# Crossing the inner layer's pieces two visits later, and multiplying two down chunks by turns

## The reference

```
h2 = rms_norm_2(x, norm2_w[l])
x = x + (silu(h2 @ w_ffn_gate[l]) * (h2 @ w_ffn_up[l])) @ w_ffn_down[l]
return rms_norm_2(x, norm_f_w)
```

## Time and profile before

| | |
|---|---|
| median of 3 runs | 2250.62 us (2250.55 to 2250.92) |
| profiled execution | 2248.62 us, its span 2247.3 us |
| TensorE busy | 2215.1 us, 99% of the span |
| DVE busy | 1532.2 us, 68% |
| ACT busy | 1217.1 us, 54% |
| mean transfer rate | 190 GB/s |

### The profile page before, as it was taken

How to read it: one execution, slowest core, us unless ns; L and a number is a source line. 1 busy time by engine, 2 the same in 40 slices (tenths; PEclk the granted TensorE clock), 3 DMA queues, 4 the chain that set the end, 5 groups by cost and what they waited for, 6 DMA issues and landing times.

```text
span 2247.3 us, 29098 instructions
## 1 busy us (share of the span) xinstructions
PE 2215.1 (99%) x11384; PEld 1826.7 (81%) x11384; DVE 1532.2 (68%) x2032; ACT 1217.1 (54%) x1681; POOL 115.3 (5%) x101
## 2 busy tenths in 40 slices
PE   9999999999999999999999999999999999999998
PEld 7888888888888887878788888887887888788776
DVE  5677765757765677675665556768886488855875
ACT  5546665646665654554454555555554345544553
POOL 0003210002220121000000000000000000000000
PEclk9999999999999999999999999999999999999999
DMA  7456676656686764445644456666756656665663
GB/s 259 145 169 182 188 211 224 206 169 195 185 242 206 215 188 137 147 131 169 206 150 152 148 170 223 212 210 185 236 188 208 198 183 207 212 208 182 192 226 131
DMA packets 311305, 426.79 MB, mean 190 GB/s; under 512 B 118976, under 2 KB 119136, under 8 KB 311040
## 3 DMA queue, kind: packets, MB, share of 16 engines
q1 hardware_dynamic: 309008, 417.82, 58.6%
q0 software_dynamic: 1584, 6.16, 0.9%
q10 hardware_dynamic: 576, 0.95, 0.1%
HBM read 396.06 MB, written 2.10 MB: 177 GB/s over the span
## 4 chain that ended last, share of the span: by engine, by line
PE 87%; DVE 5%; issue 3%; ACT 3%; DMA 2%; POOL 1%; SPq 0%; DVEq 0%; ACTq 0%; POOLq 0%
PE ACC L1091 21%; PE ACC L1093 20%; PE ACC L1092 20%; PE ACC L983 3%; PE ACC L984 3%; PE ACC L985 3%; PE SCPV L983 2%; PE SCPV L985 2%; PE SCPV L984 2%; DVE WL L2216 2%; ACT WH L1120 1%; ACT arena L1120 1%; PE SCPV L605 1%; DMA W<-in_a_w_in 0%; PE SCPV L998 0%
## 5 line engine op out<-in xcount | busy, mean ns | idle before, releaser
L2216 DVE TENSOR_TENSOR WL<-W,WH 128x1024 fp32r<-128x1024 f32 x729 | 895.2, 1236 | 423.6 <-PE ACC L1093 187.7
L1120 ACT ACTIVATE WH<-W 128x1024 fp32r<-128x1024 f32 x729 | 745.3, 1050 | 267.5 <-PE ACC L1093 128.6
L1091 PE MATMUL ACC<-WH,XH 128*128 128x512 f32 x1888 | 765.3, 405 | 3.3 <-ACT arena L1120 2.4
L1093 PE MATMUL ACC<-WH,XL 128*128 128x512 f32 x1888 | 737.6, 391 | 0.0
L1092 PE MATMUL ACC<-WL,XH 128*128 128x512 f32 x1888 | 735.9, 390 | 0.0
L1091 PEld LDWEIGHTS ACC<-WH,XH 128*128 128x128 f32 x1888 | 355.0, 188 | 80.2 <-issue 5.1
L1093 PEld LDWEIGHTS ACC<-WH,XL 128*128 128x128 f32 x1888 | 354.4, 188 | 76.2
L1092 PEld LDWEIGHTS ACC<-WL,XH 128*128 128x128 f32 x1888 | 355.4, 188 | 68.8 <-issue 1.2
L1091 PE MATMUL ACC<-WH,HH 128*128 128x512 f32 x328 | 129.5, 395 | 3.2 <-DVE HL L1663 2.1
L1092 PE MATMUL ACC<-WL,HH 128*128 128x512 f32 x328 | 128.3, 391 | 0.0
L1093 PE MATMUL ACC<-WH,HL 128*128 128x512 f32 x328 | 128.1, 390 | 0.0
(11 more groups left out here) (368 smaller groups left out, 2392.5 us busy)
## 6 DMA issues: line engine op xcount, KB each, us to landing
W<-in_w_in SPq DMA_DIRECT2D x84, 1024.0 KB, 5.0
W<-in_a_w_in SPq DMA_DIRECT2D x47, 1024.0 KB, 5.2
W<-in_w_ffn_gate SPq DMA_DIRECT2D x44, 1024.0 KB, 5.9
W<-in_w_ffn_up SPq DMA_DIRECT2D x44, 1024.0 KB, 5.3
W<-in_w_ffn_down SPq DMA_DIRECT2D x44, 1024.0 KB, 5.1
W<-in_b_w_in SPq DMA_DIRECT2D x40, 1024.0 KB, 5.2
W<-in_a_w_out SPq DMA_DIRECT2D x16, 1024.0 KB, 5.9
W<-in_b_w_out SPq DMA_DIRECT2D x16, 1024.0 KB, 6.3
```

The source lines that it names most:

```text
L1091: MM(out, hx, WH[:, k, 0:ch.width], start=q == 0 and k == 0, stop=False)
L1093: ins = MM(out, lx, WH[:, k, 0:ch.width], start=False, stop=last and k == QK - 1)
L1120: return nc.scalar.activation(out, in_, func, **how)
L2216: TT(tiles_of(M.WL[K.pair(n)], ch, half), raw, tiles_of(M.WH[n % 3], ch, half).bitcast(F32), ALU.subtract).then_inc(*did("weights_rest", n ...
```

## The change

`halves` of the feed-forward pieces starts at the fourth visit behind its piece's chunk instead of the second, and `joined` at the eleventh instead of the ninth. Through the formula above the crossing moves one load back in SP's order. The first two down chunks of each part become one chunk `d.p{p}c01` of twice the quads: for each piece of the part first the quad of the columns 0 to 511, which accumulates in ACC0 and ACC1, then that of the columns 512 to 1023, in SC0 and SC1. So a piece is first wanted two quads after the one before it, not one. The last piece crosses by DMA like the others. The squares and gains of the final norm for the first two column groups start behind the joint chunk, one visit apart.

```
-BY_DMA = {... "h0.d": range(4), "h1.d": range(4), "h2.d": range(2)}
+FF_STARTS = (0, 4, 8)
+BY_DMA = {... "h0.d": range(4), "h1.d": range(4), "h2.d": range(3)}
...
-        for c in range(NC_D):
-            add(f"d.p{p}c{c}", one("w_ffn_down_2", c * CH), "dve", quads=n, row0=done * CH, xs="H", fresh=f"h{p}.d" if c == 0 else None)
+        add(f"d.p{p}c01", one("w_ffn_down_2", 0), "both", quads=2 * n, row0=done * CH, xs="H", fresh=f"h{p}.d")
+        for c in (2, 3):
+            add(f"d.p{p}c{c}", one("w_ffn_down_2", c * CH), "dve", quads=n, row0=done * CH, xs="H")
...
-                begin(after(f"d.gu{done + j}") + 1, "halves", f"h{p}.d", j)
-                begin(after(f"d.gu{done + j}") + 8, "joined", f"h{p}.d", j)
+                begin(after(f"d.gu{done + j}") + 3, "halves", f"h{p}.d", j)
+                begin(after(f"d.gu{done + j}") + 10, "joined", f"h{p}.d", j)
...
-    for c in range(NC_D - 1):
-        begin(after(f"d.p2c{c}"), "squares", "f", c)
-        begin(after(f"d.p2c{c}") + 3, "gained", c)
+    for c, n in ((0, "d.p2c01"), (1, "d.p2c01"), (2, "d.p2c2")):
+        begin(after(n) + c % 2, "squares", "f", c)
+        begin(after(n) + 3 + c % 2, "gained", c)
...
+                        if j in FF_STARTS[1:]:
+                            pe.wait_ge(*at("acc_taken_dve", f"d.p{FF_STARTS.index(j) - 1}c1", t))
...
+    def both(ch, visit, taken):
+
+        hi, lo, last_pair = M.hi["H"], M.lo["H"], FF_STARTS[int(ch.name[3])] + ch.quads // 2 - 1
+        for q in range(ch.quads):
+            n, kq, c = ch.first + q, q // 2, q % 2
+            WH, WL = M.WH[n % 3], M.WL[K.pair(n)]
+            for half in range(QK // HK):
+                pe.wait_ge(*at("weights_rest", n, half))
+                if c == 0:
+                    pe.wait_ge(*at("turned", ch.fresh, 2 * kq + half))
+                for t in range(TB):
+                    if q == 0 and half == 0:
+                        pe.wait_ge(*at(*taken[t], t))
+                    if q == 1 and half == 0:
+                        pe.wait_ge(*at("up_taken", last_pair, t))
+                    out = (M.ACC, SC)[c][t][:, :]
...
+            visit = both(ch, visit, taken)
+            taken = [("acc_taken_dve", ch.name[:-2] + "0")] * TB
...
+    def both_taken(ch, c, t):
+        dve.wait_ge(*at("multiplied", ch.first + ch.quads - 2 + c, 1, t))
+        x = M.X[:, t, c * CH:(c + 1) * CH]
+        TT(x, (M.ACC, SC)[c][t][:, :], x, ALU.add).then_inc(*did("acc_taken_dve", f"{ch.name[:-2]}{c}", t))
...
+                    if ch.taker == "both" and q >= ch.quads - 2 and half == 1:
+                        both_taken(ch, q % 2, t)
```

More of the change, by code:

```diff
@@ L38 @@
 FF_PARTS = (4, 4, 3)
+FF_STARTS = (0, 4, 8)
 WARM = (10, 22)
-BY_DMA = {key: range(NC_D) for key in ("go.a", "x.b", "go.b", "x.c", "mx.c", "x.d")} | {"h0.d": range(4), "h1.d": range(4), "h2.d": range(2)}
+BY_DMA = {key: range(NC_D) for key in ("go.a", "x.b", "go.b", "x.c", "mx.c", "x.d")} | {"h0.d": range(4), "h1.d": range(4), "h2.d": range(3)}
 PROBS_SPLIT, PROBS_READ = 8, 17
@@ L480, in sp_program @@
                 sp.wait_ge(*at("weights_rest", n - 3, 1))
-            row = ch.row0 + (q // 2 if ch.taker == "pair" else q) * QK * P
+            row = ch.row0 + (q // 2 if ch.taker in ("pair", "both") else q) * QK * P
             place = 0
-            for w, col, width in [("w_ffn_up_2", *ch.parts[0][1:])] if ch.taker == "pair" and q % 2 else ch.parts:
+            second = {"pair": [("w_ffn_up_2", *ch.parts[0][1:])], "both": [("w_ffn_down_2", CH, CH)]}
+            for w, col, width in second[ch.taker] if ch.taker in second and q % 2 else ch.parts:
                 src = a[w][0][row:row + ch.tiles * P, col:col + width].rearrange("(k p) n -> p k n", p=P)
@@ L1032, in pair @@
         return visit + 1
+    def both(ch, visit, taken):
[13 more added lines that the diff above has]
+                    out = (M.ACC, SC)[c][t][:, :]
+                    for k in range(half * HK, (half + 1) * HK):
+                        x = kq * QK + k
+                        hx, lx = hi[:, x, t * P:(t + 1) * P], lo[:, x, t * P:(t + 1) * P]
+                        MM(out, hx, WH[:, k, :], start=x == 0, stop=False)
+                        MM(out, hx, WL[:, k, :], start=False, stop=False)
+                        ins = MM(out, lx, WH[:, k, :], start=False, stop=x == ch.quads // 2 * QK - 1)
+                    ins.then_inc(*did("multiplied", n, half, t))
+                    sides_of(tasks, K.starts, visit, live)
+                    visit += 1
+        return visit
     visit, taken = 0, [None] * TB
@@ L1075, in pe_program @@
             taken = [("gate_taken", int(ch.name[4:]))] * TB
+            continue
+        if ch.taker == "both":
+            visit = both(ch, visit, taken)
+            taken = [("acc_taken_dve", ch.name[:-2] + "0")] * TB
             continue
```

## The result

The changed kernel takes 2229.5 us in the median (2228.49 to 2230.15, 4 runs) against 2250.59 us before (2249.37 to 2250.92, 4 runs): a ratio of 0.9907, with a 95% interval of 0.989 to 0.9924. The forecast was 2231.4, in a range of 2229.5 to 2240, so the median lies on the lower end of the range; two of the four runs (2228.49 and 2229.42) lie under it. The profiled execution took 2230.15 us, the most of the four; its span is 2228.8.

The account below looks back on a forecast made before the run. TensorE, busy 99% of the span, was taken to bound the kernel. Savings of 8.2 + 2.6 + 0.4 + 8.0 = 19.2 us gave 2229.4, plus 2.0 for the median: 2231.4 us, range 2229.5 to 2240.

Parts of the forecast that it names:

- What bounds: TensorE, busy 99% of the span, bounds the kernel at 0.2267 us per matmul; only its standing still or added work matters.
- Edit one: Halves two visits later lets ACT round the third quad first; ten TensorE waits for the weights' rest go, 8.2 us.
- The crossing behind a load: On SP's queue the crossing, one load later, lands 5.5 us after issue, within margins of 2.4 and 1.8 us; cost 0.
- the serial bound: Crossing served only after the load ahead has wholly landed: 1660.25 us behind piece 2, still costing nothing by the margins.
- Edit two: Two down chunks by turns: two waits for HL go, 2.6 us, and slower starts at chunk changes, 0.4 us.
- Edit three: Last piece crossing by DMA removes TensorE's 5.5 us wait, eight transposes and slow clock; 8.0 us together.
- The sum: All gains on TensorE together: 8.2 + 2.6 + 0.4 + 8.0 = 19.2 us.
- The last step, from 2229.4 to 2231.4: Turned the profiled execution's forecast into the runs' median by adding the 2.0 us it lay above before.
- the range that I called likeliest: The forecast case's own range for the median, 2230 to 2233 us; chance 0.77.
- The weights' rest that stays late: Rival: another wait takes over in the third quads, so the halves shift gives 0, total 2239.6 us; chance 0.07.
- the waits that hid something slower: Rival: TensorE's waits were cover for something slower, such as the loads, so no change; chance 0.04.
- The slow load: Rival: each crossing waits for a load landing 8.5 us after issue, costing 28 us, total 2259; chance 0.03.

Follow-up runs that it names:

- e1: Kernel before with nothing but halves and joined two visits later; 2245.23 us, ratio 0.9979.
- e3: Changed kernel with halves and joined of the inner layer back at the second and ninth visit; 2238.97 us, ratio 0.9948.
- e5: Changed kernel with halves at the third visit instead of the fourth and joined at the tenth; 2229.04 us, ratio 0.9908.
- e8: Changed kernel with halves at the sixth visit instead of the fourth and joined at the thirteenth; 2228.99 us, ratio 0.9907.
- e7: Changed kernel with the inner layer's crossings taken by SP one load later still, behind two loads; 2264.07 us, ratio 1.0059.
- e2: Changed kernel keeping the joint chunks alone: halves and joined where they were before, last piece turned by TensorE; 2246.99 us, ratio 0.9985.
- e4: Changed kernel with the last piece turned by TensorE again, at the second visit behind its chunk; 2237.98 us, ratio 0.9943.
- e6: Changed kernel with the last piece turned by TensorE at the tenth visit behind its chunk; 2229.6 us, ratio 0.991.

## Why the prediction was right

**What bounds.** The pace of 0.2267 us from start to start held through every variant wherever the clock was granted in full, so that losses could be counted place by place. This was the step on which all else stood.

**Edit one, 8.2 us.** Shown by e1 (all ten waits go) and e3 (they come back, with an eleventh): 9.1 us at 11 places, 0.83 each where I had 0.82. The cause is the order on ACT, as e5 beside e3 shows: with the crossing where it had been in SP's order and `halves` only one visit later the gain is the same. The weights' rest had 1.5 us to spare, for 1.4 worked out.

**The crossing behind a load, 0.** Shown: e5 puts it ahead of the load again and is no faster. In the change the crossings landed after 4.7 to 6.3 us, where I took 5.5 and set 6.9 as the bound. Behind piece 2 `HL`'s first half ended at 1660.82 + 0.65 = 1661.5, 2.9 us before the fifth quad (1664.37). At the last piece, where `HL` is wanted that early, the margin was 2.6 us; I had 1.8:

```profile
2173.44 1.28 DVE L1699 TENSOR_TENSOR HL<-turning,HH 128x512 fp32r<-128x512 f32 x2
...
2176.72 0.39 PE L1058 MATMUL ACC<-WH,HH 128*128 128x512 f32 x1
```

The Trainium skill says that a queue's descriptors are taken in ring order on each DMA engine ("DMA: Bandwidth & Descriptors", Queues, rings and completion order). The medians fit that: 4.3 us with no load close ahead (e5) and behind one 3.6 us old (e8), 4.8 behind one 2.4 us old, 8.7 behind two. But the serial bound, which the prediction drew from that rule, did not hold in the change: by it the crossing behind piece 2 would have landed at 1650.23 + 5.3 + 4.3 = 1659.8, and it landed at 1657.4. The order costs nothing in the change because of the margin; in e7 it costs everything that was gained and more.

**Edit two, 3.0 us.** e2: 2.8 in the runs, 2.5 in the trace. That the last pieces' wait grows when the shift is made without the joint chunk is e1's. The edits need each other: edits one and two together, which is e4, gave 11.9 us, while each alone gave 4.6 and 2.8.

**Edit three, 8.0 us.** e4: 8.5 from median to median (2237.98 less 2229.5), 9.2 when each is taken against its own runs of before (21.1 less 11.9), 9.4 in the trace. The part that varies is how long the clock stays low. e6 splits it.

**The sum.** 19.2 us forecast, 19.7 in the trace's stretch, 21.1 in the medians. The profiled executions' stretches agree with the sum to half a microsecond. The other 1.4 us of the medians was not located: the layers ahead vary without a change (the first `pair` chunk starts between 1512.8 and 1514.9 us in the kernels here), but in the two profiled executions they go the other way, 1.2 us later after the change. The interval of the ratio, 17 to 25 us, takes in all three figures.

**The last step, from 2229.4 to 2231.4.** This is what failed in the forecast. I added 2.0 us because the median of the runs of before lay that far above its profiled execution. In the changed kernel the median lies 0.65 us below the profiled execution. I had no reason for that offset in the kernel, and it didn't carry over. So the mechanism and its sum were right, but the range that I called likeliest, 2230 to 2233, missed, and the stated range holds the median only at its very end; that it does is luck.

**The rivals.** The weights' rest that stays late and the waits that hid something slower did not happen. The slow load did not happen either, but e7 made its like by hand. I had put the point from which the change loses at a landing about 10 us after issue, which is 20.0 us behind the chunk's start, and priced each place at its wait. In e7 the crossings landed 19.3 us (piece 1) and 21.1 us (piece 2) behind it. The idling was what that arithmetic gives, 21.6 us over eleven places or 2.0 each, where I had 1.9. The price was too small all the same, since it left the clock out: a third of e7's loss is clock, so the change would lose from an earlier landing than I said.

## What to carry to other kernels

In an engine's hand-written order, look for the first operation that waits for another engine, and ask which operations stand behind it that could have run: moving the waiting one past a single rounding was worth 8 us here, at each of the three visits tried. Where an operand comes late and PSUM banks are free, two consumers can be interleaved over them; that doubled the time until the next piece is wanted, and no cost could be seen. A wait on TensorE should be priced with the slow clock behind it when it is as long as those that brought it here (2.46 us and more), and a short transfer on a queue should be placed by what stands just ahead of it.

## What the runs showed of the hardware that was not expected

- **Waits of about 2.5 us were enough to bring the low clock.** The kernel before showed it after 5.5 us only. In e1 it came after both waits for `HL`, 2.69 us (a granted clock of 0.50 for 6.1 us) and 2.46 us; in e7 after all six waits from 2.47 to 3.39 us, and after none of the five from 0.91 to 1.26 us; nor did it follow the wait of 1.45 us in the kernel before. No wait between 1.45 and 2.46 us occurred in this layer. The Trainium skill ("TensorE: Matmul & The Clock Gate", Part 1) says that the slow state is the default and activity lifts it. The rows agree in one thing: the full clock came back while TensorE was multiplying without a gap, in e1 after 6.1 us.
- **The issue of a crossing takes longer when a load was issued just ahead.** DMA_TRANSPOSE held SP's queue for 1.7 to 2.0 us with none close ahead (2.0 in the earlier trace rows), 3.0 to 3.1 us behind a load 2.4 us old, and 5.1 to 5.4 us behind two. In the change and in e7 the issue ended within 0.5 us of the landing of the load ahead, at each of the 22 crossings (1655.7 and 1655.5 behind piece 2 in the change, 1664.3 and 1664.4 in e7). Why was not tested. The next load waits for that too: it leaves 3.06 us behind the crossing in the change, 5.23 in e7.
